# A two-block transformer layer on one core: the gated MLP's root ahead of the copies of V, and x loaded in two halves around the index weights

## The reference

```python
h = x @ w_in                                  # 3112 columns: a_u, a_v | b_q, b_k, b_v | c_q, c_k, c_v | i_q, i_k, i_w
# A: gated MLP over blocks of 128 tokens
u, v = gelu(a_u), gelu(a_v)
v = layer_norm(v, ln_g, ln_b)                 # per group of 64 features: mean, variance, root
out_a = u * (w_s_masked @ v + b_s)
# B: differential attention over b_q, b_k, b_v
# C: sparse attention; which 256 keys a token sees is told by index scores:
idx_logits = einsum('bthd,bsd->bths', i_q, i_k)     # 8 heads of 32
score = einsum('bth,bths->bts', i_w * idx_scale, relu(idx_logits))
_, sel = top_k(score, 256)
x = layer_norm(ALPHA * x + concat(out_a, out_b, out_c) @ w_out, ln1_g, ln1_b)
# then an FFN, and the whole second layer
```

## Time and profile before

| | |
|---|---|
| median of 3 runs | 3107.83 us (3106.03 to 3108.56) |
| the profiled execution | 3105.51 us |
| its span | 3103.8 us |
| PE busy | 2968.8 us, 96% |
| weight loads of PE busy | 2203.5 us, 71% |
| DVE busy | 1343.7 us, 43% |
| POOL busy | 1389.8 us, 45% |
| ACT busy | 632.4 us, 20% |
| mean granted clock of PE | 0.984 |
| index products begin / end | 30.60 / 74.8 us |
| products for V end, gated product begins | 419.4, 429.4 us |
| first attention begins | 436.25 us |

### The profile page before, as it was taken

The page is one execution under the profiler, slowest core; times in us unless marked ns, Lnnn a source line. Parts: engine busy times, 40 slices in busy tenths (PEclk is TensorE's granted clock), DMA queues, the critical chain, the costliest instruction groups (busy, mean ns, idle before and its releaser), DMA issues.

```text
span 3103.8 us, 33232 instructions
## 1 busy us (share of the span) xinstructions
PE 2968.8 (96%) x13502; PEld 2203.5 (71%) x13509; DVE 1343.7 (43%) x2012; ACT 632.4 (20%) x1056; POOL 1389.8 (45%) x814
## 2 busy tenths in 40 slices
PE   7999989889999999999999898999998999999997
PEld 4544447567888888888788556667667888887886
DVE  0499957646523325334414663111413423234323
ACT  1411036521100001111211462101212211111111
POOL 2000000045666666765777003444445666666663
PEclk8999999999999999999999999999999999999999
DMA  4111126232333333333433002332333233333331
GB/s 99 34 34 34 41 81 190 80 124 82 95 109 97 94 102 95 124 95 95 122 90 101 8 1 61 82 124 66 93 106 108 89 102 91 102 93 122 95 102 62
DMA packets 364919, 273.22 MB, mean 88 GB/s; under 512 B 14048, under 2 KB 334816, under 8 KB 364768
## 3 DMA queue, kind: packets, MB, share of 16 engines
q1 hardware_dynamic: 357568, 253.30, 28.5%
q10 hardware_dynamic: 4720, 10.68, 0.9%
q0 software_dynamic: 2480, 7.13, 0.8%
HBM read 262.59 MB, written 8.49 MB: 87 GB/s over the span
## 4 chain that ended last, share of the span: by engine, by line
PE 88%; DVE 4%; DMA 3%; issue 2%; POOL 2%; ACT 1%; SPq 0%; DVEq 0%; ACTq 0%; POOLq 0%
PE PS L811 39%; PE PS L823 24%; PE PS L763 5%; PE PS L777 4%; DMA ring<-in_w_in 3%; PE PS L446 3%; PE PS L1015 2%; PE PS L883 2%; PE PS L464 2%; PE PS L484 1%; POOL w_low L1885 1%; PE PS L476 1%; PE PS L897 1%; DVE arena L552 1%; PE PS L978 1%
## 5 line engine op out<-in xcount | busy, mean ns | idle before, releaser
L1885 POOL TENSOR_TENSOR w_low<-ring,w_high 128x1024 fp32r<-128x1024 f32 x382 | 937.9, 2455 | 31.8
L1882 POOL TENSOR_SCALAR w_high<-ring 128x1024 fp32r<-128x1024 f32 x382 | 425.7, 1114 | 1024.6 <-PE PS L823 372.1
L823 PE MATMUL PS<-w_high,hid_high 128*128 128x512 f32 x864 | 337.2, 390 | 9.1 <-issue 9.1
L823 PE MATMUL PS<-w_high,hid_low 128*128 128x512 f32 x864 | 336.7, 390 | 0.0
L823 PE MATMUL PS<-w_low,hid_high 128*128 128x512 f32 x864 | 336.6, 390 | 0.0
L811 PE MATMUL PS<-hT_high,w_high 128*128 128x512 f32 x656 | 271.9, 414 | 14.0 <-POOL w_low L1885 14.0
L811 PE MATMUL PS<-x1T_high,w_high 128*128 128x512 f32 x704 | 275.6, 391 | 3.5 <-DVE x1T_low L1576 3.5
L811 PE MATMUL PS<-x1T_low,w_high 128*128 128x512 f32 x704 | 275.0, 391 | 0.0
L811 PE MATMUL PS<-x1T_high,w_low 128*128 128x512 f32 x704 | 274.9, 390 | 0.0
L811 PE MATMUL PS<-hT_high,w_low 128*128 128x512 f32 x656 | 256.8, 391 | 0.0
L811 PE MATMUL PS<-hT_low,w_high 128*128 128x512 f32 x656 | 256.5, 391 | 0.0
(11 more groups left out here) (268 smaller groups left out, 4616.7 us busy)
## 6 DMA issues: line engine op xcount, KB each, us to landing
ring<-in_w_ff SPq DMA_DIRECT2D x128, 512.0 KB, 3.8
ring<-in_w_in SPq DMA_DIRECT2D x112, 512.0 KB, 3.9
ring<-in_w_gu SPq DMA_DIRECT2D x88, 512.0 KB, 3.8
ring<-in_w_ada SPq DMA_DIRECT2D x48, 512.0 KB, 5.1
ring<-in_w_down SPq DMA_DIRECT2D x44, 512.0 KB, 3.6
ring<-in_w_out SPq DMA_DIRECT2D x32, 512.0 KB, 4.4
ring<-in_w_branch SPq DMA_DIRECT2D x16, 512.0 KB, 3.9
arena<-in_x SPq DMA_DIRECT2D x8, 512.0 KB, 8.9
```

Of the source, the lines that this page charges most:

```text
L823: mm = pe.matmul(PS[:, 2 * p + half, :], x[:, k, at], w[:, q, half_of(half)], start=(first and n == 0), stop=(last and n == 2))
L1882: pool.tensor_scalar(w_high[:, q, :], ring[:, s, :], 1.0, 1.0, ALU.mult, ALU.mult).then_inc(weights_high, 1)
L1885: pool.tensor_tensor(w_low[:, q, :], ring[:, s, :], w_high[:, q, :].bitcast(F32), ALU.subtract).then_inc(weights_used[s], 1)
```

## The change

There are two edits. ACT's wait for `gmlp_var` and its root move from behind the four copies of "bv" to ahead of them. And x comes in two halves: "turn_x" and "idx" are now two stages each. SP issues x 0 to 3, index tiles 0 and 1, x 4 to 7, and then the key's tile. PE transposes blocks 0 to 3, waits for ACT's copies of them, multiplies tiles 0 and 1 with tokens 0 to 511, transposes blocks 4 to 7 (into the two PSUM pairs that the open products don't hold), waits for their copies, multiplies tiles 0 and 1 with tokens 512 to 1023, and then tile 2 with both halves. ACT's order is the same as before in this part, only the names of the units differ.

```diff
-    "turn_x": ([], [None] * NB),
+    "turn_x": ([], [None] * 4),
     "cqk": (whole(2), [0, 1]),
-    "idx": ([(1, False), (1, False), (4, False)], [0, 1, 2]),
...
-ORDER = [("turn_x", 0), ("idx", 0), ("cv", 0), ("cqk", 0), ("score", 0), ("cqk", 1), ("auv", 0), ("turn_ws", 0),
+ORDER = [("turn_x", 0), ("idx", 0), ("turn_x", 1), ("idx", 1), ("cv", 0), ("cqk", 0), ("score", 0), ("cqk", 1), ("auv", 0), ("turn_ws", 0),
...
-PAIRS_OF = {("cqk", 0): (3,), ("score", 0): (0, 1, 2), ("cqk", 1): (0, 1)}
+IDX = [(whole(2), [0, 1]), (whole(1, 4), [0])]
+PAIRS_OF = {("turn_x", 1): (2, 3), ("idx", 1): (2,), ("cqk", 0): (3,), ("score", 0): (0, 1, 2), ("cqk", 1): (0, 1)}
...
             pe.wait_ge(ident_made, 2)
-            for b in range(NB):
-                p = L.pair("turn_x", 0, b)
+
+            def turn_x(b):
+                p = L.pair("turn_x", b // 4, b % 4)
                 pe.wait_ge(x_loaded[b], 16)
-                pair_here(pe, "turn_x", 0, b)
+                pair_here(pe, "turn_x", b // 4, b % 4)
                 for k in range(KT):
                     mm = pe.transpose(PS[:, 2 * p + k // 4, (k % 4) * P:(k % 4 + 1) * P],
                                       x_tok[:, b, k * P:(k + 1) * P], ident[:, :])
                 mm.then_inc(psum_full[p], 1)
-            all_pairs_free(pe, "idx")
-            by_feature(pe, "idx", 0, xT)
+
+            def idx(c, h):
+                i = c // 2
+                s, p = L.slot("idx", i, c % 2), L.pair("idx", i, c % 2)
+                if h == 0:
+                    weights_here(pe, "idx", i, c % 2)
+                    pair_here(pe, "idx", i, c % 2)
+                for k in range(KT):
+                    mm = pe.matmul(PS[:, 2 * p + h, :], ring[:, s, k * P:(k + 1) * P], xT[:, k, half_of(h)],
+                                   start=(k == 0), stop=(k == KT - 1))
+                if h == 1:
+                    mm.then_inc(weights_used[s], 1)
+
+            for b in range(4):
+                turn_x(b)
+            for b in range(4):
+                freed(pe, "turn_x", 0, b)
+            for c in range(2):
+                idx(c, 0)
+            for b in range(4, NB):
+                turn_x(b)
+            for b in range(4):
+                freed(pe, "turn_x", 1, b)
+            for c in range(2):
+                idx(c, 1)
+            for h in HALVES:
+                idx(2, h)
             by_token(pe, "cv", xT, 264)
...
             copy_features("bqk", 1, bqkT, 4)
+            act.wait_ge(gmlp_var, 1)
+            act.activation(vstat[:, 1, :], vstat[:, 1, :], ACT.Sqrt).then_inc(gmlp_sqrt, 1)
             for u in range(4):
                 p = L.pair("bv", 0, u)
                 unit_here(act, "bv", 0, u)
                 act.copy(bv[:, 2 * u:2 * u + 2, :], pair(p)).then_inc(psum_free[p], 1)
-            act.wait_ge(gmlp_var, 1)
-            act.activation(vstat[:, 1, :], vstat[:, 1, :], ACT.Sqrt).then_inc(gmlp_sqrt, 1)
...
-            for b in range(NB):
+            rows = w1.rearrange("(k p) n -> p k n", p=P)
+
+            def load_x(b):
                 sp.dma_start(x_tok[:, b, :], t["x"][0, tok(b), :]).then_inc(x_loaded[b], 16)
-            rows = w1.rearrange("(k p) n -> p k n", p=P)
+
+            for b in range(4):
+                load_x(b)
             for c in range(2):
                 feature_tile_load("idx", 0, c, w1, I_Q + c * P)
-            slot_free("idx", 0, 2)
-            dst = ring[:, L.slot("idx", 0, 2), :].rearrange("p (k n) -> p k n", k=KT)
+            for b in range(4, NB):
+                load_x(b)
+            dst = ring[:, L.slot("idx", 1, 0), :].rearrange("p (k n) -> p k n", k=KT)
             for r in range(4):
-                load("idx", 0, 2, dst[:, :, 32 * r:32 * r + 32], rows[:, :, I_K:I_K + 32])
+                load("idx", 1, 0, dst[:, :, 32 * r:32 * r + 32], rows[:, :, I_K:I_K + 32])
```

More of the change, by code:

```diff
@@ L139, in __init__ @@
         for stage, i in ORDER:
-            chunks, units = STAGES[stage]
+            chunks, units = STAGES[stage] if stage != "idx" else IDX[i]
             self.pairs_at[stage, i] = list(pairs)
@@ L888, in _ @@
             for c in range(3):
-                freed(pe, "idx", 0, c)
+                freed(pe, "idx", c // 2, c % 2)
             step = 0
@@ L1130, in _ @@
             for b in range(NB):
-                p = L.pair("turn_x", 0, b)
-                unit_here(act, "turn_x", 0, b)
+                p = L.pair("turn_x", b // 4, b % 4)
+                unit_here(act, "turn_x", b // 4, b % 4)
                 act.copy(xT[:, :, tok(b)], flat(p).rearrange("p (k n) -> p k n", k=KT)).then_inc(psum_free[p], 1)
@@ L1138, in _ @@
             for c in range(3):
-                p = L.pair("idx", 0, c)
-                unit_here(act, "idx", 0, c)
+                p = L.pair("idx", c // 2, c % 2)
+                unit_here(act, "idx", c // 2, c % 2)
                 act.copy(iqT[:, c, :] if c < 2 else ikT[:, :], flat(p)).then_inc(psum_free[p], 1)
```

## The result

The changed kernel takes 3076.84 us (median of 4 runs, 3071.79 to 3078.41), the kernel before 3107.57 (4 runs). The ratio is 0.9899, with a 95% interval of 0.9882 to 0.9916: 30.7 us faster. The forecast was 20.0 us, 3087.8, and the range ended at 3081.5. In two later measurements the same two kernels stood 23 and 25 us apart. Of the 7.5 us between 30.7 and 23, 3.9 lie in the kernel before, whose median was 3103.68 there; the experiments show what may be behind another part.

What follows compares the result with a forecast made beforehand. PE bounds the kernel, so only its standing still or lower clock matters. Root 11.75 us plus start 8.2 us make 20.0 us, from the median 3107.83 to 3087.8 us; range 3081.5 to 3096.

Steps and rivals of the forecast that it cites:

- What bounds the kernel: Whole kernel: PE, busy 2968.8 of 3103.8 us; only its standing still or lower clock matters, at start and gated MLP.
- The root: Gap before the gated MLP's product: with ACT's root ahead of V's copies, the first attention starts 11.75 us earlier.
- The start: x in two halves: V of the sparse attention starts at 66.6 us instead of 74.8, 8.2 us saved.
- T: Landing time of weight tile 0 at the start, taken as 17.0 us; the saving was 25.2 minus this time.
- the clock's fall: First index products: PE idles before them, so its clock is low and 2.9 us are lost.
- blocks and copy: Between the half-0 and half-1 products: four x blocks 4.4 us and ACT's last copy 1.1, no longer hidden, 5.5 us.
- cap of 13: Start: the saving can't exceed 13 us, because x 7's landing near 32 us then binds.
- The lower bound: Earliest landing of tile 0: it takes block 4's place byte for byte and lands at 12.9 us.
- (b): Rival at the start: queue 0's constants go first, tile 0 lands at 22 to 30 us; 3093 to 3101 us; chance 0.19.
- (c): Rival at the gated MLP: its gap doesn't close, the product waits on "issue"; 3099 to 3103 us; chance 0.05.
- (d): Rival, slower: SP is held at weight issues, x 4 to 7 start late; chance 0.03 with all other mishaps.
- eighth of x's bytes per turn: DMA queues at the start: weight rows of 512 bytes against x's 4096 give a tile an eighth per turn.

Runs made afterwards that it cites:

- constants_late: The kernel before with the root moved, x in the old order, and POOL's constants held back until the last x block landed: 3073.69 us, ratio 0.9904.
- root_only: The kernel before with only the root moved ahead of the copies of V: 3089.75 us, ratio 0.9961.
- tiles_behind_5: The changed kernel with one more block of x (x 0 to 4) issued ahead of index tiles 0 and 1: 3086.01 us, one run.

## Why the prediction was wrong

**What bounds the kernel** held: both gaps of PE went, and the time with them.

**The root** came out as written: 11.6 us for 11.75. ACT's root followed the variance 0.03 us after DVE's instruction ended, so the table load went ahead of the wait; V's copies still waited 10.88 us for PE; the gated product ran 3.60 us for 3.44; the attention started 5.1 us behind V's end (409.31 against 404.19), as the terms 3.44 and 1.68 gave.

**The start** failed by one term, T, the landing of weight tile 0, and by the clock's fall that hung on it. The steps: T 17.0, measured 11.2, so early that PE waited for ACT's copy instead, until 12.12; the clock's fall 2.9 us, measured 0, since PE stood still for only 1.41 us ahead of the products; half 0 13.7 us, measured 14.1 without PE's wait for tile 1; x 4 to 7 all there when wanted, in truth PE waited 0.91 us for tile 1 and 0.78 for x; blocks and copy 5.5 us, measured 33.23 - 27.11 = 6.1; half 1 and tile 2 27.5 us, measured 27.5. Saved 14.0 for 8.2, slightly over the cap of 13 that the text gave, since x 7 was there at 30.9 instead of 32.

Why T was wrong: I set tile 0's landing from how long a weight tile took when it stood behind x 7, in the middle of the constants, and put this 8.0 us behind x 3, at a time when hardly any constant was moving. In the trace of the changed kernel only queue 0's first transfer, c (landed by 9.6 us), came before tile 0's end; the next, b_ada, landed at 15.8. The trace of before had the same two transfers of queue 0, c landing at 10.5 us and b_ada at 16.3. I took the time of contention from 9.7 us as given and didn't set against it how short a tile's own time is: without the constants 1.8 us (13.45 to 15.27 in constants_late). Ten of tile 0's 16 shares were down by 10.4 us. The lower bound, 12.9 us from block 4, wasn't a bound either: in root_only, with x in the same order, block 4 landed at 10.7 us. One execution had been taken for the kernel.

Yet 17.0 is near what happens when the last of 16 shares is late, in two of six traces (16.55 and 16.98), and then the whole sum of the start is right within 0.1 us. For T that is luck: the prediction let the whole tile be slow, and in these traces 15 shares were there by 12.7 and 11.7. The terms behind T, the clock's fall among them, are borne out by it. So a better forecast has two values for the start, 14 and 8.3 us, and not one with a range around it. This may be a part of why the changed kernel gained 30.7 us in one measurement and 23 and 25 in two others; how often each start occurs was not measured. The clock also dips in later stages, at places that differ from trace to trace; what share of the spread that makes was not measured either.

**The rest**: 1.3 us in and around the score stage and 1.5 in the second layer, together somewhat more than the 2 us that the text left for the clock; they lie on the fast side. 14.0 + 11.6 + 1.3 + 1.5 make 28.4 us, and less than 0.2 went in the stages between: the 28.3 of the two profiles. The medians are 2.4 us further apart, since the profiled execution of before lay 2.1 us below its median and that of after 0.4 above. Without the 5.8 us that the start gave over its 8.2, the time would have been inside the range.

**Rivals.** (b) did not come as such: tile 1 was held up beside the constants (8.9 us behind tile 0, at 114 GB/s), but it is wanted only when tile 0's products are done, 7.1 us after they begin, so this cost 0.91 us. (c) fell. (d) fell: one issue of x held SP for 3.76 us, and PE waited 0.78 us for x.

On the rule of the Trainium skill (DMA: Bandwidth & Descriptors, Queues, rings and completion order), that engines change queues packet by packet: the traces agree that a small queue can hold up a large one. Beside the constants, tile 1's 512 KB took 8.9 us, and without them tile 1 landed 1.8 us behind tile 0. No run here tells turns by packet from turns by another unit. The prediction's eighth of x's bytes per turn, its own reckoning, doesn't show as an eighth of the speed: where b_ada was moving, 512 KB of tile 0 took 8.9 us (10.68 to 19.57 in tiles_behind_5) and 512 KB of x 4.7 (12.92 to 17.61 in before).

## What to carry to other kernels

Before moving a large transfer in a crowded queue, look for the small ones beside it: holding back 17 constants of 0.5 MB in all let x land 9 us earlier (13.5 against 22.4), and this one wait on POOL gave the start more than a reordering of PE, SP and two planner stages. When a transfer's place is moved, date the contention by landings on the other queue, and if the moved one ends close to where it begins, forecast two cases. And where an engine's small step waits behind copies that themselves wait, its place in line is the whole cost: in every trace with the root ahead of the copies it is 5.3 us from the gated product to the attention.

## What was not expected of the hardware

A transfer is as late as its last share: 15 shares of tile 0 landed by 11.7 us and the sixteenth at 17.0, with the same code that elsewhere landed all by 11.2, and PE's products waited for the sixteenth (17.22). And queue 0's 0.21 MB cost queue 1 more than its 25.7% tells: without it the same engines moved 390 GB/s instead of 158.
